# Two weight chunks of a wide round by seven block products instead of eight, their sums on GpSimd

## The reference

```python
def swiglu(h, w_in, w_out):
    gu = h @ w_in                       # (256 x 2048) @ (2048 x 11264)
    gate, up = gu[..., :D_FF], gu[..., D_FF:]
    return (jax.nn.silu(gate) * up) @ w_out   # (256 x 5632) @ (5632 x 2048)

h = h + 0.5 * swiglu(rmsnorm(h, ffn1_norm[l]), ffn1_w_in[l], ffn1_w_out[l])
...   # mixer of the first block
h = h + 0.5 * swiglu(rmsnorm(h, ffn2_norm[l]), ffn2_w_in[l], ffn2_w_out[l])
```

## Time and profile before

| what | value |
|---|---|
| time, median of 3 runs (lowest to highest) | 2704.01 us (2703.9 to 2704.29) |
| span of the profiled execution, first to last instruction | 2702.0 us |
| share of the span: PE, weight loads, DVE, ACT, POOL | 100%, 82%, 58%, 48%, 2% |
| mean DMA rate | 204 GB/s |
| granted TensorE clock | 1.000 |

### The profile page before, as it was taken

How to read it: one execution, slowest core, us unless ns; L and a number is a source line. 1 busy time by engine, 2 the same in 40 slices (tenths; PEclk the granted TensorE clock), 3 DMA queues, 4 the chain that set the end, 5 groups by cost and what they waited for, 6 DMA issues and landing times.

```text
span 2702.0 us, 34407 instructions
## 1 busy us (share of the span) xinstructions
PE 2690.3 (100%) x12194; PEld 2223.4 (82%) x12194; DVE 1573.3 (58%) x1960; ACT 1303.8 (48%) x1730; POOL 58.2 (2%) x64
## 2 busy tenths in 40 slices
PE   9999999999999999999999999999999999999999
PEld 7888888888888788888888888887888888888887
DVE  6555555555744466555555555668556586566566
ACT  6443444344544455443444344555554464575463
POOL 0000000000000000000000000030000000021000
PEclk9999999999999999999999999999999999999999
DMA  9876677666745477766676666764457576546754
GB/s 309 267 217 195 209 215 215 194 213 200 251 155 164 147 223 223 218 217 202 202 219 216 197 209 202 230 215 158 148 176 251 162 223 228 179 141 206 237 180 137
DMA packets 422280, 550.59 MB, mean 204 GB/s; under 512 B 40992, under 2 KB 267552, under 8 KB 421376
## 3 DMA queue, kind: packets, MB, share of 16 engines
q1 hardware_dynamic: 420352, 539.90, 64.1%
q0 software_dynamic: 1648, 8.86, 1.0%
q10 hardware_dynamic: 144, 0.04, 0.0%
HBM read 525.59 MB, written 23.07 MB: 203 GB/s over the span
## 4 chain that ended last, share of the span: by engine, by line
PE 98%; DMA 1%; SPq 0%; DVE 0%; ACT 0%; issue 0%; ACTq 0%; DVEq 0%
PE bank L1391 31%; PE bank L1393 31%; PE bank L1392 31%; DMA raw<-in_ffn_w_in_dram 1%; PE bank L1350 1%; PE bank L1087 0%; PE bank L839 0%; PE bank L823 0%; PE bank L1067 0%; PE bank L521 0%; PE bank L793 0%; SPq L1268 0%; PE bank L533 0%; PE bank L830 0%; DVE wlo L1741 0%
## 5 line engine op out<-in xcount | busy, mean ns | idle before, releaser
L1741 DVE TENSOR_TENSOR wlo<-raw,whi 128x1024 fp32r<-128x1024 f32 (+2 forms) x975 | 1151.2, 1186 | 1067.4 <-ACT whi L1476 1062.4
L1476 ACT CAST whi<-raw 128x1024 fp32r<-128x1024 f32 (+2 forms) x975 | 986.3, 1016 | 1280.0 <-PE bank L1393 1268.5
L1391 PE MATMUL bank<-whi,p_hi 128*128 128x512 f32 x2016 | 789.4, 392 | 3.3 <-DVE wlo L1741 3.3
L1393 PE MATMUL bank<-whi,p_lo 128*128 128x512 f32 x2016 | 785.1, 389 | 0.0
L1392 PE MATMUL bank<-wlo,p_hi 128*128 128x512 f32 x2016 | 784.9, 389 | 0.0
L1391 PE MATMUL bank<-whi,q_hi 128*128 128x512 f32 x1696 | 664.6, 392 | 0.5 <-DVE wlo L1741 0.5
L1393 PE MATMUL bank<-whi,q_lo 128*128 128x512 f32 x1696 | 660.6, 390 | 0.0
L1392 PE MATMUL bank<-wlo,q_hi 128*128 128x512 f32 x1696 | 660.3, 389 | 0.0
L1391 PEld LDWEIGHTS bank<-whi,p_hi 128*128 128x128 f32 x2016 | 378.5, 188 | 84.6 <-issue 6.0
L1393 PEld LDWEIGHTS bank<-whi,p_lo 128*128 128x128 f32 x2016 | 378.5, 188 | 79.0
L1392 PEld LDWEIGHTS bank<-wlo,p_hi 128*128 128x128 f32 x2016 | 378.7, 188 | 77.7 <-issue 0.2
(11 more groups left out here) (298 smaller groups left out, 1025.9 us busy)
## 6 DMA issues: line engine op xcount, KB each, us to landing
raw<-in_ffn_w_in_dram SPq DMA_DIRECT2D x704, 256.0 KB, 3.1
raw<-in_ffn_w_out_dram SPq DMA_DIRECT2D x320, 256.0 KB, 3.3
raw<-in_w_in_a_dram SPq DMA_DIRECT2D x192, 256.0 KB, 3.1
raw<-in_w_in_mix_dram SPq DMA_DIRECT2D x128, 256.0 KB, 3.1
raw<-in_w_ple_gate_dram SPq DMA_DIRECT2D x128, 256.0 KB, 3.8
raw<-in_w_in_b_dram SPq DMA_DIRECT2D x128, 256.0 KB, 3.1
raw<-in_w_out_mix_dram SPq DMA_DIRECT2D x64, 256.0 KB, 3.3
raw<-in_w_o_a_dram SPq DMA_DIRECT2D x64, 256.0 KB, 3.8
```

Of the source, the lines that this page charges most:

```text
L1391: pe.matmul(o, xht, wh, start=(kt == t_first), stop=False)
L1393: ins = pe.matmul(o, xlt, wh, start=False, stop=(kt == t_last))
L1476: act.copy(whi[:, c % SPLIT, 0:n, 0:w], raw[:, c, 0:n, 0:w]).then_inc(hi_done, 1)
L1741: dve.tensor_tensor(wlo[:, c % SPLIT, 0:n, 0:w], raw[:, c, 0:n, 0:w], whi[:, c % SPLIT, 0:n, 0:w].bitcast(F32), ALU.subtract).then_inc(lo_ ...
```

## The change

Most rounds of the two nets are joined in pairs: a wide round computes 1024 output columns. In an `in` stage these are 512 gate and 512 up columns, in an `out` stage 1024 neighbouring columns. Wide are three of four pairs in `in0` (its first two rounds stay), all of `in1`, the first two of three in `in2`, and both in `out0` and `out1`: 13 in each net, 26 in all. A wide round uses banks 0 to 3 at once and has 16 units; a unit is two K tiles of one half of the columns, again 12 matmuls, with the buffers of a chunk.

In K chunks 2 and 5 of a wide round (`SEVEN`) the 2x2 block product (2 token tiles by 2 K tiles, times 2 K tiles by 2 column halves) is computed by Strassen's scheme in Winograd's form: seven products of three matmuls instead of eight. Four of them need sums of weight tiles, which POOL adds, ACT casts and DVE subtracts; four need sums of activation tiles, which DVE and ACT make once for a stage that shares them. The four products that enter several outputs collect in banks 4 to 7, are combined by DVE into `parts_out`, and are added when the banks are emptied. The hardware loops are gone.

```diff
+SEVEN = (2, 5)
...
+                wide = ((1, 2, 3), (0, 1, 2, 3), (0, 1))[g]
+                into.rounds = [(k, None) for k in range(n) if k // 2 not in wide]
+                into.rounds = sorted(into.rounds + [(2 * r_, r_) for r_ in wide], key=lambda r_: r_[0])
+                if g < 2:
+                    back.rounds = [(2 * r_, r_) for r_ in range(2)]
...
+                def load_wide(wide):
+                    halves = halves_behind(s, wide)
+                    for i in range(2 * CH):
+                        sp.wait_ge(lo_done, unit_at(s, wide, i) + 1)
+                        if unit_at(s, wide, i) - CH in summed_units:
+                            sp.wait_ge(t24_sum, summed_units[unit_at(s, wide, i) - CH] + 1)
...
+                        for s_, k_ in halves:
+                            if i == 12:
+                                store_hidden(s_, k_, k_ % 2)
+                            if i == 15:
+                                move_hidden(s_, k_, k_ % 2)
...
+            def weight_sums(s, wide, c):
+                q = seven_number(s, wide, SEVEN.index(c))
+                if q:
+                    pool.wait_ge(t13_used, q)
+                    pool.wait_ge(t24_used, q)
+                a_ = 2 * c % CH
+                for n in range(2):
+                    pool.wait_ge(landed[a_ + n], (s.r0 + 2 * wide + 2 * c // CH) * 32 + 32)
+                b12 = raw[:, a_ + 1, 1, :]
+                pool.tensor_tensor(w_sums[:, 0, :], raw[:, a_, 0, :], b12, ALU.add)
+                pool.tensor_tensor(w_sums[:, 1, :], raw[:, a_ + 1, 0, :], b12, ALU.add).then_inc(t13_sum, 1)
...
+                pool.tensor_tensor(w_sums[:, 2, :], w_sums[:, 1, :], raw[:, a_, 0, :], ALU.add).then_inc(sem("t2_sum"), 1)
...
+                pool.tensor_tensor(w_sums[:, 3, :], w_sums[:, 2, :], raw[:, a_, 1, :], ALU.add).then_inc(t24_sum, 1)
...
+                def seven_products(wide, c, sums):
...
+                    product(p1, *split_x(2 * c, 0), *split_w(2 * c, 0), first, last_)
+                    product(sums[0][0][:, :], *split_x(2 * c + 1, 0), *split_w(2 * c, 1), False, False).then_inc(chunk_used, 1)
+                    pe.wait_ge(lo_done, unit_at(s, wide, 2 * c + 1) + 1 + LO0)
+                    product(sums[1][0][:, :], *s3, *split_w(2 * c + 1, 0), False, False).then_inc(chunk_used, 1)
+                    pe.wait_ge(t13_lo, q + 1)
+                    product(p5, *s5, *t1, first, last_)
+                    product(p7, *s7, *t3, first, last_).then_inc(t13_used, 1)
+                    pe.wait_ge(t24_lo, q + 1)
+                    ins = product(p6, *s6, *t2, first, last_)
...
+                    product(sums[0][1][:, :], *split_x(2 * c + 1, 1), *t4, False, False).then_inc(t24_used, 1)
...
+            def wide_round(s, wide):                 # ACT
+                n = wides.index((s.name, wide))
+                for c in range(2, CH):
+                    wide_hi(s, wide, 2 * c)
+                    if c == CH - 1:
+                        act.wait_ge(p_full, n + 1)
...
+                        act.copy(parts_out[:, 0, :], bank[4][:, :]).then_inc(p1_out, 1)
+                    wide_hi(s, wide, 2 * c + 1)
+                    if c in SEVEN:
+                        weight_sums_hi(s, wide, SEVEN.index(c))
...
+                    if c == 4:
+                        for s_, k_ in halves_behind(s, wide):
+                            hidden_hi(s_, k_, k_ % 2)
...
+            def operand_sums(s, i):
...
+                link(dve.tensor_tensor(a_.rearrange("p (k n) -> p k n", k=2), pair_hi[s.pair][:, kt:kt + 2, :].bitcast(F32),
+                                       pair_lo[s.pair][:, kt:kt + 2, :].bitcast(F32), ALU.add))
+                a11, a21, a12, a22 = (a_[:, n * P:(n + 1) * P] for n in range(4))
+                dve.tensor_tensor(whole[:, i, 2, :], a11, a21, ALU.subtract)
+                link(dve.tensor_tensor(whole[:, i, 0, :], a22, a21, ALU.subtract))
+                link(dve.tensor_tensor(whole[:, i, 1, :], whole[:, i, 0, :], a11, ALU.add))
+                dve.tensor_tensor(whole[:, i, 3, :], a12, whole[:, i, 1, :], ALU.subtract).then_inc(op_sum, 1)
...
+            def combine_products(s, wide):
...
+                link(dve.tensor_tensor(y_, p1, p6, ALU.subtract))
+                dve.tensor_tensor(w_, y_, p5, ALU.add)
+                link(dve.tensor_tensor(x_, y_, p7, ALU.add))
+                link(dve.tensor_tensor(y_, w_, p7, ALU.add))
...
+            def begin_wide(s, wide, before):         # DVE
+                for i in range(2):
+                    wide_lo(s, wide, i)
+                if before[2] is None:
+                    evacuate(before[0], before[1], before[1] % 2)
+                else:
+                    evacuate_wide(before[0], before[2])
+                for i in range(2, 4):
+                    wide_lo(s, wide, i)
...
+                    if s.name[-3:] == "in0" and k == 1:
+                        for i in range(2):
+                            operand_sums(s, i)
+                        for i in range(2):
+                            operand_sums_lo(s, i)
...
-                paired_rounds(dve, s, round_)
+                for k, wide in s.rounds:
```

More of the change, by code:

```diff
@@ L104, in __init__ @@
         self.after = None
+        self.rounds = [(k, None) for k in range(n)]
     def chunk_tiles(self, c):
@@ L120, in __init__ @@
         self.number = None
[L123 to L131, removed]
 def build(nc, A, out, upto=None):
@@ L272, in build, with after, ahead_of, seven_number @@
         last = stages[-1]
+        flat = [(s, k, wide) for s in stages for k, wide in s.rounds]
+        wides = [(s.name, wide) for s, k, wide in flat if wide is not None]
+        def after(s, k):
+            n = [(q.name, k_) for q, k_, _ in flat].index((s.name, k))
+            return flat[n + 1] if n + 1 < len(flat) else None
+        def ahead_of(s, k):
+            n = [(q.name, k_) for q, k_, _ in flat].index((s.name, k))
+            return flat[n - 1] if n else None
+        def seven_number(s, wide, i):
+            return 2 * wides.index((s.name, wide)) + i
         GAIN = dict(ffn1=0, mix=16, ffn2=32, final=48, pool=64, gla=72)
@@ L332, in hidden_behind @@
         def hidden_behind(s, k, u, peeled, behind):
+            if s.kind == "ffn_in" and k >= behind and s.rounds[-1][1] is None and k == 4:
+                return None
+            if s.kind == "ffn_in" and k == 5 and behind == 2:
+                return None
             if s.kind == "ffn_in" and not (peeled and k < behind):
@@ L338, in hidden_behind, with halves_behind @@
             return None
+        def halves_behind(s, wide):
+            before = ahead_of(s, 2 * wide)
+            if before is None or before[0].kind != "ffn_in" or before[2] is None:
+                return ()
+            return (before[0], before[1]), (before[0], before[1] + 1)
         def turned_behind(s, k, peeled, behind):
@@ L447, in round_before, with unit_at, unit_tiles, split_tiles @@
             return q.name, q.n - 1
+        def unit_at(s, wide, i):
+            return (s.r0 + 2 * wide) * CH + i
+        summed_units = {unit_at(s, wide, 2 * c + n): seven_number(s, wide, i) for s, _, wide in flat if wide is not None
+                        for i, c in enumerate(SEVEN) for n in range(2)}
+        def unit_tiles(i):
+            return (2 * (i // 2), 2 * (i // 2) + 1) if i % 2 == 0 else (2 * (i // 2) + 1, 2 * (i // 2))
+        def split_tiles(i):
+            return 1 if i % 2 and i // 2 in SEVEN else 2
+        def operand_number(s, i):
+            return 6 * (s.name[3] == "2") + (i + 1 if s.kind == "ffn_in" else 3 + 2 * int(s.name[-1]) + i)
         def sums_done(eng, s, k):
@@ L1460, in _ @@
+                for k, wide in s.rounds:
+                    if wide is None:
+                        round_(k, k % 2)
+                    else:
+                        wide_round(wide)
         @block.scalar
@@ new lines, in operand_sums_hi, with wide_silu @@
+            def operand_sums_hi(s, i):
+                whole, sum_hi, _ = sums_of[s.kind]
+                act.wait_ge(op_sum, operand_number(s, i))
+                act.copy(sum_hi[:, i, :, :], whole[:, i, :, :]).then_inc(op_hi, 1)
+            def wide_silu(s, wide):
+                act.wait_ge(acc_free, s.a0 + 2 * wide + 1 + FREE0)
+                for t in range(TT):
+                    ins = act.activation(sg[:, :, t, :], sg[:, :, t, :], ACT.Silu, scale=rstd[:, t:t + 1])
+                ins.then_inc(silu_done, 1)
@@ L1652, in first_half @@
                         block_hi(*block)
+                    if s.kind == "ffn_in" and k == 5 and c == 3:
+                        for k_ in (2, 3):
+                            hidden_hi(s, k_, k_ % 2)
                     if peeled and s.r0 + k:
@@ L1935, in first_half @@
                         block_lo(*block)
+                    before = ahead_of(s, k)
+                    if before and before[2] is not None and c == 1:
```

(6 more changed lines are left out.)

287 lines of the change are left out of this document (256 added, 31 removed).

## The result

The changed kernel takes 2716.19 us (median of 4, 2714.47 to 2716.94) against 2703.99 us: a ratio of 1.0044, 95% interval 1.003 to 1.0059. It is 12.2 us slower, where 14.0 us less were forecast. The 156 matmuls are worth 35.4 us; 47.6 us came back, where 21.4 were forecast.

A forecast was written before the change was run, and what follows sets the result against it. The prediction took PE, busy 100% of the span, as the bound, so matmul count and operand arrival decide. Its terms, -35.4 + 7.0 + 14.4 = -14.0 us, gave 2690.0 us from 2704.0, range 2669 to 2714.

The forecast's parts named there:

- What goes: Chunks with seven products in 26 wide rounds: 156 matmuls fewer, 35.4 us, all on the path.
- The first wide round: First wide round in `in0` of each net: PE stalls 3.5 us for DVE's subtraction, +7.0 us in all.
- the walk to 1082.5: At `in0`: activation sums, casts and unit 0's subtraction end at 1082.5, PE arrives at 1079.0; 3.5 us stall.
- 5 us if they meet POOL's sums: Upper bound on the stall at each net's first wide unit; lower bound 2 us, 3.5 taken.
- rows 7: Profile rows cited for POOL's sums beside DVE: a subtraction took 1.99 us instead of 1.23.
- Rounds that bring pieces back: 16 wide rounds returning two pieces: PE stalls near unit 10 or round end, 0.9 us each, +14.4 us.
- The forecast's own sign of being wrong: In rounds returning pieces: the forecast is wrong if the moves land beyond 6 us, against 5.3 taken.
- The end of the round: DVE empties banks late after a return round's last subtractions; POOL's sums on three of them add 2.3 us.
- What costs nothing: Ten other wide rounds, the `band` cast, 2 KB load rows and POOL's mixer DMAs: no added time.
- full lockout: Last three subtractions of 16 rounds each wait 1.30 us for POOL's sums: +13.2, 2717 us; chance 0.09.
- The slower rival: Moves landing after 6.5 us hold ACT before unit 10, 3.3 us late in 16 rounds: 2729 us; chance 0.08.

## Why the prediction was wrong

*What goes:* right. 156 matmuls, and with nearly all waits gone 32.1 of 35.4 us appear.

*The first wide round:* right in place and cause, wrong in size, 16.4 instead of 7.0 us. Three steps failed, and the first hid part of the second.

The arrival of PE was read one chunk too early. ACT's cast at 1079.22 is the third of the new round; it follows PE's leaving chunk 6 of the round before, and at 1079.0 PE still has chunk 7 to do. The same matmul that is the first of unit 0 in the changed kernel, counted from the start of the program, stands here in the kernel before:

```profile
1081.68 0.39 PE L1391 MATMUL bank<-whi,q_hi 128*128 128x512 f32 x1
```

So the walk to 1082.5 gives 0.8 us in the second net, not 3.5. In the first net the piece was finished at 52.04 and PE came at 54.91, and the same walk gives 3.7. Without collisions the term is 4.5 us for both, not 7.0.

The bound "5 us if they meet POOL's sums" was too low: it leaves 1.5 us for collisions, twice the 0.76 that rows 7 show on one subtraction. The 3.7 us for DVE's sums were right where POOL is silent (3.6 us). But an operation waits for what is left of POOL's, however short it is itself: 0.9 to 1.1 us each. Ten operations stand in a row there beside four sums of POOL, and in each net four of them were caught: 7.7 us instead of 3.7. With 4.0 us more, the walks give 7.7 and 4.8 us; PE waited 7.2 and 4.0 by the distance of its starts. When POOL's sums start could have been walked through like the return round.

A price not in the forecast at all is the clock: after these two waits PE ran 22 matmuls at 1.2 GHz, 4.4 us.

*Rounds that bring pieces back:* right in place (unit 10), cause (ACT behind the moves) and number (16, and none in the others), wrong in size, 1.94 instead of 0.9 us each. The walk gave 0.8 us at unit 10 with a landing of 5.3; issue was 0.4 us later and travel 0.4 us longer in the mean, and PE waited 1.44 us. Then came 0.2 us at half clock and 0.3 us in small pieces elsewhere in the round. The failed step is the value taken: the wait at unit 10 was mis-sized (0.8 us, 1.44 measured), and the total of the walk, 2.1 us, was talked down to 0.9 with overlaps of DVE that do not reach unit 10. That 2.1 lies near the measured 1.94 is luck: 1.3 of it was lateness at the end of the round, which did not come. At a dead heat an error in one direction costs its full size and in the other nothing, so the expected loss lies above the one computed at the middle; I treated it as if it could average out. The forecast's own sign of being wrong, moves that land beyond 6 us, came in 5 of the 16 rounds (up to 6.7).

*The end of the round:* the collisions there (2.3 us forecast at most) hardly count. Without the wait at unit 10, with all sums in place, the 16 rounds lose 0.12 us each.

*What costs nothing:* right. (What DVE gains in a wide round adds up to 6.3 us from the rows, not 6.6; nothing hangs on it, and its share is 70% as forecast.) The other wide rounds lose 0.1 us each, PE waits for no weight sum, and the layout without the seven products is at 1.0007.

*Rivals:* full lockout gave 2717 us and the time came to 2716, but not by its mechanism: its waits were to stand at the last subtractions of the 16 rounds, where there are none. Its rule did hold at the starts, within 0.14 us. So the near hit is luck. The slower rival named the right mechanism (ACT in front of unit 10) with a point of decision at 1.8 us per round; 1.94 were measured, and the range ended 2 us below the time.

## What to carry to other kernels

An engine that waits in order for a distant result belongs behind what the bottleneck needs next: moving one line, without a faster operation anywhere, was worth 30 us here. Where a walk through a round ends in a dead heat, price it by the spread of the latest arrival and not by its middle, and look for the edit that takes it off the edge. When a second engine is given work, ask what stands beside it at that moment, and count its collisions per operation and not per microsecond. And before a stall is worked out from a cast or a load, check which chunk's release it waited for: buffers run ahead, here by four chunks.

## What the hardware showed that was not expected

An operation of DVE on 128x128 took 0.29 us alone and 1.23 to 1.40 us beside a 128x512 sum of POOL, and two subtractions took 4.52 us instead of 2.35 beside POOL's sums in a row.

The granted clock fell to 1.2 GHz after some of PE's waits and not after others: after 7.2, 4.0, 2.0 and 2.2 us (by the distance of starts) in the changed kernel, and not after one of 2.9 and another of 2.2 us. In its wide rounds 37 matmuls ran with starts 0.43 us apart, 7.4 us more than at full clock; with the waits gone the mean clock is 1.000 again. What decides which wait has this effect stays open.
